# A two-layer hybrid decoder on one core: the end of the mixer loop and the opening are put in another order

## The reference

```
h = rms_norm(x, norm_mix); u = h @ w_in
y = [rms_norm(mla(u), g0), rms_norm(nsa(u), g1), rms_norm(lru(u), g2), ssd(u)]   # 4 groups of 256 columns
x = x + y @ w_out
x = x + ffn(rms_norm(x, norm_ffn))
# rms_norm(y, g) = y * rsqrt(mean(y*y) + 1e-6) * g
# lru: log_a = -8 r softplus(-lam); b = sqrt(-expm1(2 log_a)) * (i * x); h = scan(a h + b); h * gelu(gate)
```

## Time and profile before

| | |
|---|---|
| three runs | 1519.02, 1519.4, 1522.42 us; median 1519.4 |
| the profiled execution | 1522.7 us, its span 1520.8 us |
| TensorE busy | 1487.0 us, 98% of the span |
| VectorE, ScalarE busy | 1218.0 us (80%), 1004.1 us (66%) |
| mean granted clock of TensorE | 0.995 |

### The profile page before, as it was taken

One profiled execution on the slowest core, in us unless ns is written; L12 is line 12 of the kernel. 1 busy time (PEld: TensorE's weight loads), 2 busy tenths in 40 slices (PEclk: granted clock), 3 DMA queues, 4 the chain that ended last, 5 costly groups with the idle time before them and its releaser, 6 DMA issues.

```text
span 1520.8 us, 19966 instructions
## 1 busy us (share of the span) xinstructions
PE 1487.0 (98%) x7379; PEld 1246.2 (82%) x7379; DVE 1218.0 (80%) x1279; ACT 1004.1 (66%) x890; POOL 77.5 (5%) x124
## 2 busy tenths in 40 slices
PE   7999999999999999999999999999999999999997
PEld 6987888888798788878888888888888888888885
DVE  6678644544667889998899889888989889889986
ACT  6476544333547677777777777777777778778764
POOL 3101000000000020000000000000000000000000
PEclk9999999999999999999999999999999999999998
DMA  9804655555440269999999999999999999999991
GB/s 318 246 1 128 220 190 176 194 188 191 167 139 1 84 244 393 396 343 394 394 352 388 394 364 377 396 389 349 394 395 346 394 396 342 395 397 346 393 396 76
DMA packets 189963, 444.22 MB, mean 292 GB/s; under 512 B 9713, under 2 KB 15998, under 8 KB 189902
## 3 DMA queue, kind: packets, MB, share of 16 engines
q1 hardware_dynamic: 185350, 427.81, 76.7%
q0 software_dynamic: 4528, 15.58, 3.9%
q10 hardware_dynamic: 24, 0.01, 0.0%
HBM read 435.51 MB, written 7.86 MB: 292 GB/s over the span
## 4 chain that ended last, share of the span: by engine, by line
PE 93%; DVE 3%; ACT 2%; issue 1%; DMA 0%; SPq 0%; POOLq 0%; DVEq 0%; POOL 0%; ACTq 0%
PE bank L457 27%; PE bank L458 27%; PE bank L456 27%; PE bank L589 3%; PE bank L515 2%; PE bank L592 1%; PE bank L703 1%; PE bank L751 1%; ACT w_hi L1337 0%; PE bank L761 0%; PE bank L720 0%; PE bank L977 0%; DMA work<-in_nsa_cmp_pe_dram 0%; PE bank L621 0%; ACT work L1493 0%
## 5 line engine op out<-in xcount | busy, mean ns | idle before, releaser
L1822 DVE TENSOR_TENSOR w_lo<-ring,w_hi 128x2048 fp32r<-128x2048 f32 x372 | 846.5, 2290 | 177.0 <-ACT w_hi L1364 176.4
L1364 ACT ACTIVATE w_hi<-ring 128x2048 fp32r<-128x2048 f32 x372 | 712.0, 1916 | 223.3 <-PE bank L456 223.3
L457 PE MATMUL bank<-w_hi,xT_hi 128*128 128x512 f32 x896 | 353.7, 395 | 0.0
L458 PE MATMUL bank<-w_hi,xT_lo 128*128 128x512 f32 x896 | 349.5, 390 | 0.0
L456 PE MATMUL bank<-w_lo,xT_hi 128*128 128x512 f32 x896 | 240.2, 390 | 0.0
L457 PE MATMUL bank<-w_hi,hidT_hi 128*128 128x512 f32 x560 | 220.8, 394 | 2.7 <-DVE hidT_lo L1829 2.7
L458 PE MATMUL bank<-w_hi,hidT_lo 128*128 128x512 f32 x560 | 218.3, 390 | 0.0
L456 PEld LDWEIGHTS bank<-w_lo,xT_hi 128*128 128x128 f32 x896 | 168.2, 188 | 35.7
L458 PEld LDWEIGHTS bank<-w_hi,xT_lo 128*128 128x128 f32 x896 | 168.5, 188 | 33.7
L457 PEld LDWEIGHTS bank<-w_hi,xT_hi 128*128 128x128 f32 x896 | 168.3, 188 | 33.6
L457 PE MATMUL bank<-w_hi,hT_hi 128*128 128x512 f32 (+2 forms) x384 | 149.9, 393 | 6.9 <-DVE hT_lo L1777 2.7
(11 more groups left out here) (386 smaller groups left out, 1261.6 us busy)
## 6 DMA issues: line engine op xcount, KB each, us to landing
ring<-in_moe_w_gate_dram SPq DMA_DIRECT2D x112, 1024.0 KB, 9.4
ring<-in_moe_w_up_dram SPq DMA_DIRECT2D x112, 1024.0 KB, 9.4
ring<-in_moe_w_down_dram SPq DMA_DIRECT2D x112, 1024.0 KB, 9.0
ring<-in_ffn_w_gate_dram SPq DMA_DIRECT2D x14, 1024.0 KB, 5.1
ring<-in_ffn_w_up_dram SPq DMA_DIRECT2D x14, 1024.0 KB, 5.1
ring<-in_ffn_w_down_dram SPq DMA_DIRECT2D x14, 1024.0 KB, 4.8
ring<-in_w_in_dram SPq DMA_DIRECT2D x12, 1024.0 KB, 7.0
ring<-in_w_out_dram SPq DMA_DIRECT2D x8, 1024.0 KB, 8.0
```

What stands on the lines that cost most here:

```text
L457: pe.matmul(o, x_hi, w, start=start, stop=False)
L458: return pe.matmul(o, x_lo, w, start=False, stop=False)
L1364: act.activation(w_hi[:, (base + at) % SPLIT, :], ring[:, i, :], ACT.Copy).then_inc(hi_ready, 1)
L1822: dve.tensor_tensor(w_lo[:, v, :], ring[:, (base + at) % RING, :], w_hi[:, v, :].bitcast(F32), ALU.subtract).then_inc(lo_ready, 1)
```

## The change

*The recurrence's root by tokens.* `lru_square` multiplies the squares (now the stationary operand) by four columns of ones: the sums stand with tokens on the partitions, 128x2 of them. VectorE adds epsilon, GpSimd raises to -1/2, VectorE makes two diagonal matrices, and TensorE spreads them over the partitions (`lru_spread`, two matmuls, in the middle of `project_output(1)`). ScalarE's second square root and VectorE's reciprocal are gone. *Turned groups weighted at eviction.* For MLA, SSD and NSA, ScalarE writes the high part straight from the bank, with the gain as its scale, and VectorE writes the low part from the same bank; the pass through yT is gone. *The first square root* stands behind the last exponentials. *Order.* Units 12 and 13 are split by ScalarE before the recurrence's high part; VectorE's outputs(6) stand behind the scan. One probability tile moves to free columns (`probT_cmp`), since the low part of MLA is written earlier. *Opening.* x is waited for by halves, unit 0 comes in two transfers with two high copies, the parameters are turned behind unit 0, ScalarE makes a first copy of one column early, TensorE makes filler matmuls (`warm_up`), and GpSimd issues the positions' transfer behind its constants. *End.* One filler matmul in each of the three passes. Lines without a change of order (new semaphores, renumbered `lru_act` waits, the removed form of the transposes and of by_token's loop) are left out.

```diff
+def probT_cmp(n):
+    return probT[:, n % 2, 7 * P:8 * P] if n == 6 else probT[:, n % 2, 0:P]
...
+def warm_up(times):
+    for _ in range(times):
+        pe.matmul(banks[5][:, 0:P], ident[:, :], ident[:, :], start=True, stop=True)
 pe.wait_ge(ident_ready, 1)
+warm_up(4)
 pe.wait_ge(mix_in, 16)
...
 give(pe.transpose(b_mix[:, 0:KT], prow[0:KT, 0, :], ident[0:KT, 0:KT]), 0)
-pe.wait_ge(x_in, 16 * TB)
 mark["raw", 0] = gave[0]
...
+for half in range(2):
+    b_x = [bank(0), bank(0)]
     for tb in range(TB):
-        turn_half(0, b_x, tb, g)
...
+        if half == 0:
+            pe.wait_ge(x_in[tb], 16)
+        for i in range(2):
+            turn_half(0, b_x[i], tb, 2 * half + i)
+warm_up(2)
+def turn_parameters():
+    pe.wait_ge(consts_ready, 1)
+    pe.wait_ge(prow_in, 16 * N_PROW)
...
+    mm.then_inc(par_turned, 1)
...
         pe.wait_ge(lo_ready, u0 + (at + 1))
+    elif isinstance(u0, int) and u0 + at == 0:
+        pe.wait_ge(first_hi, 1)
...
+                opening = p == 0 and h == 0 and not low
+                for ks in ((0, 1), (2, 3)) if opening else (range(4),):
+                    if opening and 2 in ks:
+                        pe.wait_ge(hi_ready, 1)
+                    for tb in range(TB):
+                        t = slice(tb * P, (tb + 1) * P)
+                        for k in ks:
+                            if first and tb == 0 and k % 2 == 0 and not low:
+                                pe.wait_ge(dve_took, mark["raw", 2 * l] + 2 * h + k // 2 + 1)
+                            mm = products3(b[tb][:, 0:n], hT_hi[:, 4 * h + k, t], hT_lo[:, 4 * h + k, t],
+                                           w[:, k, 0:n], h == 0 and k == 0, h == 1 and k == 3, low)
+                        if h == 1 and low and tb == 0:
+                            give(mm, 1)
             mm.then_inc(units_used, 1)
+            if p == 0 and h == 0:
+                turn_parameters()
...
-        pe.wait_ge(lru_act, 5 * l + 4)
+        pe.wait_ge(lru_act, 4 * l + 4)
         b = bank(0)
-        for i in range(2):
-            mm = pe.matmul(b[:, 0:S], ones[:, :], lt1[:, i, :], start=(i == 0), stop=(i == 1))
+        for tb in range(TB):
+            for i in range(2):
+                mm = pe.matmul(b[:, 4 * tb:4 * tb + 4], lt1[:, i, tb * P:(tb + 1) * P], ones[:, 0:4],
+                               start=(i == 0), stop=(i == 1))
         give(mm, 0)
...
+    def lru_spread():
+        pe.wait_ge(lru_diag, l + 1)
+        b = banks[(mark["lsq", l] - 1) % 4]
+        for tb in range(TB):
+            mm = pe.matmul(b[:, tb * P:(tb + 1) * P], ones[:, :], rdiag[:, tb, :], start=True, stop=True)
...
             pe.wait_ge(act_took, gave[1])
-        pe.wait_ge(yT_lo_ready, 4 * l + i + 1)
+        if i == 2:
+            pe.wait_ge(yT_lo_ready, l + 1)
+        else:
+            pe.wait_ge(dve_took, mark["yT", l, {0: 0, 1: 2, 3: 1}[i]])
         last = i == 3
...
                 turn_output(1)
+            if i == 1 and low and tb == 0:
+                lru_spread()
             w = parts_of(p, p, i, low).rearrange("p (k n) -> p k n", k=2)
...
 with pe.Fori(0, 3) as o:
+    pe.matmul(banks[0][:, 0:2 * P], ident[:, :], cbias[:, :], start=True, stop=True)
     with pe.If(novf_r > o):
...
             wait_free(p)
+            if p == 0:
+                sp.dma_start(slot_k(0)[:, 0:2, 0:UA], rows[:, 0:2, 0:UA]).then_inc(first_in, 16)
+                sp.dma_start(slot_k(0)[:, 2:4, 0:UA], rows[:, 2:4, 0:UA]).then_inc(slot_full[0], 16)
+                small_rows()
+                p += 1
+                continue
...
-pool.dma_start(pos_i[:, :], positions.rearrange("(t p) -> p t", p=P),
-               allow_slow_non_contiguous=True).then_inc(pos_in, 16)
...
 pool.wait_ge(consts_ready, 1)
+pool.dma_start(pos_i[:, :], positions.rearrange("(t p) -> p t", p=P),
+               allow_slow_non_contiguous=True).then_inc(pos_in, 16)
...
     roots(2, 2)
+    c0 = 4 * (5 * l + 3) + 2
+    pool.wait_ge(dve_took, mark["lsq", l])
+    pool.tensor_tensor(rstd[:, c0:c0 + TB], stat[:, c0:c0 + TB], minus_half[:, 0:TB], ALU.pow)\
+        .then_inc(lru_root, 1)
     roots(2)
...
+act.wait_ge(ident_ready, 1)
+act.activation(stat[:, 3:4], ident[:, 0:1], ACT.Copy)
...
+def split_first():
...
+    act.wait_ge(first_in, 16)
+    act.activation(w_hi[:, 0, 0:4 * UA // 2], slot(0)[:, 0:4 * UA // 2], ACT.Copy).then_inc(first_hi, 1)
+    act.wait_ge(slot_full[0], fills[0])
+    act.activation(w_hi[:, 0, 4 * UA // 2:], slot(0)[:, 4 * UA // 2:], ACT.Copy).then_inc(hi_ready, 1)
...
         split_turned(0, (0, 1))
-        split(p)
+        split_first()
         split_turned(0, (2, 3))
+        split(p + 1)
         for tb in range(TB):
             mean_square(0, tb, xres[:, tb, :], D, hn[:, tb, :])
-        split(p + 1)
...
+    def turned_output(i, turn):
...
+        act.wait_ge(*filled_by[0][at])
+        c0 = PR["grp"] + 2 * W_OUT_ORDER[i]
+        for k in range(2):
+            hi = act.activation(yT_hi[:, 2 * i + k, :], banks[at % 4][:, k * S:(k + 1) * S], ACT.Copy,
+                                scale=par[:, l, c0 + k:c0 + k + 1])
+        hi.then_inc(yT_hi_ready, 1)
...
+            split(p + 10)
+        if n == 7:
+            turned_output(0, 0)
+        if n == 8:
+            turned_output(1, 2)
             act.wait_ge(lru_vec, 4 * l + 3)
             act.activation(lb[:, :, :], lb[:, :, :], ACT.Sqrt).then_inc(lru_act, 1)
-            split(p + 10)
-        if n == 7:
-            act.wait_ge(dve_took, mark["yT", l, 0])
-            act.activation(yT_hi[:, 0:2, :], yT[:, 0:2, :], ACT.Copy).then_inc(yT_hi_ready, 1)
-        if n == 8:
-            act.wait_ge(dve_took, mark["yT", l, 2])
-            act.activation(yT_hi[:, 2:4, :], yT[:, 2:4, :], ACT.Copy).then_inc(yT_hi_ready, 1)
             split(p + 11)
...
-            act.wait_ge(dve_took, mark["lsq", l])
-            act.activation(lrstd[:, :], lrstd[:, :], ACT.Sqrt).then_inc(lru_act, 1)
+    act.wait_ge(*filled_by[0][mark["pv", l, len(AJ) - 1] - 1])
+    split(p + 12)
+    split(p + 13)
...
     act.activation(yT_hi[:, 4:6, :], yT[:, 4:6, :], ACT.Copy).then_inc(yT_hi_ready, 1)
-    split(p + 12)
-    split(p + 13)
-    act.wait_ge(dve_took, mark["yT", l, 1])
-    act.activation(yT_hi[:, 6:8, :], yT[:, 6:8, :], ACT.Copy).then_inc(yT_hi_ready, 1)
+    turned_output(3, 1)
...
         split_turned(0, (2, 3))
+        split(p + 1)
...
-    split(p + 1)
+    else:
+        split(p + 1)
...
-    def turned_output(grp):
+    def turned_output(i):
         b = filled()
-        at = 2 * W_OUT_ORDER.index(grp)
-        gain = par[:, l, PR["grp"] + 2 * grp:PR["grp"] + 2 * grp + 2].unsqueeze(2)\
-            .broadcast_to([P, 2, S])
-        empty_bank(dve.tensor_tensor(yT[:, at:at + 2, :],
-                                     b[:, :].rearrange("p (k t) -> p k t", k=2), gain, ALU.mult))
-    def split_output(i):
         dve.wait_ge(yT_hi_ready, 4 * l + i + 1)
-        dve.tensor_tensor(yT_lo[:, 2 * i:2 * i + 2, :], yT[:, 2 * i:2 * i + 2, :],
-                          yT_hi[:, 2 * i:2 * i + 2, :].bitcast(F32), ALU.subtract)\
-            .then_inc(yT_lo_ready, 1)
+        c0 = PR["grp"] + 2 * W_OUT_ORDER[i]
+        for k in range(2):
+            lo = dve.scalar_tensor_tensor(out=yT_lo[:, 2 * i + k, :], in0=b[:, k * S:(k + 1) * S],
+                                          scalar=par[:, l, c0 + k:c0 + k + 1],
+                                          in1=yT_hi[:, 2 * i + k, :].bitcast(F32), op0=ALU.mult,
+                                          op1=ALU.subtract)
+        empty_bank(lo)
...
-        if n >= 2:
+        if n >= 2 and n != 8:
             outputs(n - 2)
...
         if n == 7:
-            turned_output(0)
             dve.wait_ge(rstd_ready, 8 * l + 5)
...
         if n == 8:
-            split_output(0)
-            turned_output(3)
+            turned_output(0)
             split(p + 10)
-            split_output(1)
-            dve.wait_ge(lru_act, 5 * l + 3)
+            dve.wait_ge(lru_act, 4 * l + 3)
             link(dve.scalar_tensor_tensor(out=lb[:, :, :], in0=lb[:, :, :], scalar=0.5, in1=lt1[:, :, :],
...
+            outputs(6)
+            turned_output(1)
+            b = filled()
+            c0 = 4 * (5 * l + 3) + 2
+            empty_bank(dve.tensor_scalar(stat[:, c0:c0 + TB],
+                                         b[:, 0:4 * TB].rearrange("p (t q) -> p t q", t=TB)[:, :, 0], EPS,
+                                         None, ALU.add))
             split(p + 11)
-            b = filled()
-            empty_bank(dve.tensor_scalar(lrstd[:, :], b[:, 0:S], EPS, None, ALU.add))
+            dve.wait_ge(lru_root, l + 1)
+            for tb in range(TB):
+                ins = dve.tensor_scalar(rdiag[:, tb, :], ident[:, :], rstd[:, c0 + tb:c0 + tb + 1], None,
+                                        ALU.mult)
+            tell(ins, "lru_diag", lru_diag)
         if n == 9:
-            dve.wait_ge(lru_act, 5 * l + 5)
```

(12 more changed lines are left out.)

54 lines of the change are left out of this document (23 added, 31 removed).

## The result

The changed kernel takes **1512.5 us** (median of 5 runs, 1512.34 to 1513.02) beside 1520.9 for the kernel before in the same comparison (5 runs, 1519.02 to 1522.42): a ratio of 0.9946, with 0.9935 to 0.9956 as its 95% interval. The profiled execution took 1513.0 us, its span is 1511.3. The forecast was 1510.4 us in a range from 1507.8 to 1514.6, and 1513.7 for the profiled execution.

A forecast was written before the change was run, and what follows sets the result against it. TensorE, busy 98% of the span, was taken as the bound. Opening 2.6, loop ends 6.4 and end 0 sum to 9.0 us; 1519.4 - 9.0 gives 1510.4 us, range 1507.8 to 1514.6.

The forecast's parts named there:

- Steps (1) and (2): Loop end: earlier exponentials and weighed evictions start project_output(0) at 125.5, 2.2 us earlier, at the full clock.
- Steps (3) and (4): Loop end: moved square root costs a 0.55 us wait; lru_square's matmuls take 1.0; project_output(1) starts at 132.9.
- rival F: Loop ends: table switch with a drain, root 1.4 us later, 2.8 us less gained, 1513.2 us; chance 0.02.
- Step (5): Loop end, root by tokens: unit 11's split covers GpSimd's power; project_output(2) starts at 139.45, 3.2 us earlier.
- Rival B: Loop ends: the lower clock stays at project_output(0), costing 0.85 us each layer, 1512.1 us; chance 0.13.
- Opening: Kernel start: unit 3 starts 2.6 us earlier, bounds 1.7 and 3.1, with the rope chain 0.9 earlier.
- rival A: Opening: unit 0's halves land no earlier, rope chain keeps its time; 1.7 us or less, 1511.5; chance 0.16.
- End: Last eight matmuls: the lower clock falls as before, gain 0, between +0.2 and -1.0 us.
- likeliest case: Whole kernel: the forecast of 1510.4 us, with its own range 1508.4 to 1512.3; chance 0.50.
- C: Loop ends: root by tokens late, each us beyond 1.0 counts twice, 3 us late gives 1514.4; chance 0.07.
- D: Loop ends: square root's chain late at lru_square, each us counts twice, 7.0 more gives 1524.4 us; chance 0.04.
- E: Expert stage: full DMA engines bound the kernel and give nothing back, 1519.4 us; chance 0.05.

The follow-up runs named there:

- fourth experiment: Changed kernel with the square root back ahead of unit 10's copy and job 7's exponentials: 1515.3 us.
- sixth experiment: Changed kernel with ScalarE's Square ahead of lru_square made three times over, a longer chain with the same output: 1518.1 us.
- the fifth: Changed kernel with VectorE's split of unit 11 behind the root's diagonals in place of ahead of them: 1513.3 us.
- the seventh: Changed kernel with outputs(7) and unit 11's split changing places around the diagonals, and job 7's weights ahead of the mask: 1513.2 us.
- the last: Changed kernel with the rope chain late, outputs(7) ahead of the diagonals, unit 11's split behind, job 7's weights moved and the spread earlier: 1509.3 us.
- first experiment: Kernel before with the new opening alone, loop ends and last loop as before: 1519.2 us.
- the tenth: Kernel before with filler matmuls alone, in the opening and in each pass of the last loop, nothing moved: 1520.1 us.
- eighth experiment: Changed kernel with the rope chain and ScalarE's sine, exponential and logarithm moved behind early unit splits and copies: 1510.1 us.
- ninth kernel: Kernel before with the new loop ends and the last loop's filler, but the old opening: 1514.7 us.

## Why the prediction was right, and where it was off

*Steps (1) and (2), what stands ahead of project_output(0)*: forecast at 125.5 on the clock of before, it came at 125.39 (122.26 and 3.13), at the full clock. Products(6) were forecast for 124.05 and came at 123.91. The fourth experiment prices the step at 1.0 us a layer by itself (by the stretches), not at 2.2: what it wins in front is partly lost in the wait of step (3), as that step said.

*Steps (3) and (4), the root's new place and lru_square*: a wait of 0.55 was forecast, 0.54 came; 1.0 for the four short matmuls, 1.05 came; project_output(1) at 132.9, it came at 132.89. The root starts 1.29 us after the table load does (123.12 and 124.41), so rival F's drain isn't there. This agrees with the rows of before and not with the 2.66 us that the Trainium skill, ScalarE: Activation LUTs, section "What ACT_TABLE_LOAD costs", has for a switch.

*Step (5), the root by tokens*: this is the step of the loop end that was mis-sized. "GpSimd's power 0.71" took 2.67. I had given it a cover, VectorE's split of unit 11, and the cover is what slowed it: 2.67 beside the split (also in the fourth and sixth experiments, 2.68 and 2.67), 0.70 with VectorE idle or in outputs. On the clock of before the epsilon came at 132.75, as forecast, and the split ended at 135.10 (135.0), but the diagonals were done at 136.17 (135.5), after VectorE's wait of 0.59 for the power. Of these 0.67 us, 0.38 reached project_output(2): 139.83, forecast at 139.45. So a layer gave 2.7 to 2.95 in place of 3.2, 5.6 in place of 6.4, inside the bounds of 4.5 and 7.4. That the split slows the power is shown by the fifth, seventh and last kernels. What it costs the kernel is less so: with the contention gone alone the kernel was no faster (the fifth, the seventh), and only with the spread further ahead, outputs(7) as the cover and the weights moved did a layer get 0.6 to 0.7 shorter (the last).

*Rival B* was wrong in both parts. The clock did not stay low, and in the old loop end the low clock had cost nothing (111.06 us in the first kernel's profile without it, 110.98 in the tenth's with it). ScalarE's chain to project_output(2), the row that ends the wait there, set the pace. In the new loop end it would cost: 1.5 us a layer in the sixth experiment.

*Opening*: forecast 2.6 with unit 3 at 29.2; it came at 28.50, 3.26 earlier, because both halves of unit 0 were copied by 10.0 (forecast 12.0), and the rope chain ended at 23.4 (forecast 24.1). The clock, up from the first product in this profile, has little part in where the new opening ends (28.39 to 28.73 in the profiles that began at the lower one), but much in where the old one does. The reason given, that "the rope chain" stands behind it and TensorE alone would gain more, held: the eighth experiment took 2.1 us more out of it. But the 3.26 contains some 1.4 that belong to one profile of the kernel before: its opening put unit 3 at 31.76 with eleven products at the lower clock, the same opening with six of them (ninth kernel) at 30.40, and with none (tenth) at 30.16. Beside those two the new order is worth 1.9 and 1.7 us, which is what rival A had. The slack of 1.7 that the prediction gave unit 3's copy was itself read from products at the lower clock.

*End*: "0", with -1.0 as its bound, was 0.8 in the two profiles and a few tenths over the runs.

*The sum*: 9.0 was forecast, 9.7 came between the two profiled executions (9.5 by their spans). That it is so near is in part luck: the opening gave 0.7 more than forecast, the end 0.8 more, the loop ends 0.8 less. Still the median came 2.1 above the forecast, and the step that is off is the last line of the sum, 1519.4 - 9.0. I took the gain of a profiled execution of 1522.7 us off a median of three runs 3.3 below it, "in which I expect the same terms". They weren't the same. The kernel before spreads over 4.7 us in its 47 runs, 3.4 in the five of the comparison, and the changed kernel over 0.7 in five; a gain that consists partly of a restored clock can't be taken again off a run that had it. Over the 47 runs the median of before is 1521.6, and 1521.6 - 9.0 is 1512.6. The likeliest case's own range ended at 1512.3 and missed by 0.2; the full range held.

*Slips in the working*: 6.4 less 0.85 for each layer is 4.7 and not 4.5, rival A's time is 1511.3 and not 1511.5, and all gains at their upper bounds (3.1, 7.4, 1.0) give 1507.9. None of them changes a verdict.

*Rivals A, C, D and E*: the opening gave more than A's 1.7 between the two traces (3.26) and by the medians (2.2 to 2.4), but about that once the lower clock of the old opening is set aside. C came in part (0.59 us of wait for GpSimd), far from its price. D did not come: ScalarE's chain was late by the 0.54 foreseen. E is refuted by both profiles, 600.00 of 600 us.

## What to carry to other kernels

- Before taking a trace's gain off a median, look at how the runs of before spread, and at what the profiled one was: a change that restores a clock pays only in the runs that had lost it, and makes the kernel steadier as much as faster.
- A wait of half a us for another engine's chain is paid in full, and a longer one can be paid twice, if no other wait stands behind it; where another one did, as in the old loop end, the lower clock cost nothing. Ask of each stretch which chain sets its end before pricing a clock.
- When an engine's work is put "under" another's, ask what they share. The cover chosen for GpSimd's small power made it nearly four times as long.

## What the runs showed of the hardware

GpSimd's power of 128x2 values took 2.67 to 2.68 us when VectorE had begun a subtraction of two SBUF operands (128x2048, 2.28 us) 0.16 us earlier, and 0.70 to 0.72 in the other cases seen: with VectorE idle, with one operand in PSUM, or with the power begun first. In the slow case it ended 0.55 us after the subtraction: it looks as if it had waited for it. The kernel before already had a row like it at its end, a power of 128x1 that takes 0.99 us begun behind a VectorE instruction with two large SBUF operands, and 0.57 or 0.58 elsewhere. VectorE, then GpSimd:

```profile
1515.32 0.74 DVE L2507 SCALAR_TENSOR_TENSOR hn<-xres,rstd,gfin 128x512 f32<-128x512 f32 x1
```

```profile
1515.48 0.99 POOL L1292 TENSOR_TENSOR rstd<-rstd,minus_half 128x1 f32<-128x1 f32 x1 [1.01 <-DVE rstd L2502]
```

The order decides. In the changed kernel the next power begins 0.17 us ahead of a subtraction of two SBUF operands, and neither is slowed (that subtraction takes 0.68 or 0.69 elsewhere). GpSimd, then VectorE:

```profile
135.79 0.72 POOL L1267 TENSOR_TENSOR rstd<-stat,minus_half 128x2 f32<-128x2 f32 x1
```

```profile
135.96 0.69 DVE L2321 TENSOR_TENSOR hT_lo<-hT,hT_hi 128x512 fp32r<-128x512 f32 x1 [0.80 <-ACT hT_hi L1646]
```

The Trainium skill, SBUF — State Buffer, section "Who interferes with whom", says the first case in advance: a VectorE instruction with two SBUF inputs contends with a GpSimd instruction that reads SBUF, what they share is an exclusive lock, and the order of issue decides who blocks. By that rule and the rows the power would end, as an estimate, at 131.97 and 0.7, 132.7; it ended at 132.52, so the trace agrees within 0.2. In the other order no run here shows VectorE blocked. The rule was not weighed in the prediction.

TensorE's lower level came and went under the same code. Eleven and six first products were at 0.43 us in two profiles of the old opening; in ten profiles of the new one it was none in four, one or two in five and three or four in one. The same 1.30 and 1.08 us of idle time were followed by 0.43 in the earlier trace rows and by 0.23 in the first experiment; 1.86 and 1.88 ahead of lru_square by 0.23 in one layer and 0.43 in the other, in one execution. No run here shows what decides between them.
